# Reordering the first mixer and the memory attention of a two-block transformer kernel, and turning some projections round

## The reference, cut to what matters

```python
h = rms_norm(x, norm_mix[l])
z = h @ w_in[l]                      # 2048 x 5144
z_a, z_b, z_cq, z_ckv_c, z_ckv_s, z_ckv_w, z_cg = jnp.split(z, split_at, axis=-1)
out_a = spatial_gating(z_a, ...)     # gMLP
out_b = dilated_attention(...)       # 4 heads, from z_b: "attention B"
out_c = nsa_attention(...)           # 8 heads, 2 key groups, compressed keys: "attention C"
x = x + jnp.concatenate([out_a, out_b, out_c], axis=-1) @ w_out[l]
h = rms_norm(x, norm_xattn[l]); m = rms_norm(mem, norm_mem[l])
q = h @ xattn_wq[l]; kv = m @ xattn_wkv[l]        # memory attention, 4 heads: "attention X"
x = x + softmax_attention(q, kv) @ xattn_wo[l]
x = x + jnp.square(jax.nn.relu(rms_norm(x, norm_mlp[l]) @ w_up[l])) @ w_down[l]
# second block: its six modulation vectors are
jax.nn.silu(c) @ w_mod[l] + b_mod[l]              # w_mod: 2048 x 12288; the same for c_ctx
```

## Time and profile before

| what | value |
|---|---|
| median of 3 runs | 2880.22 us (2876.76 to 2888.32) |
| the profiled execution | 2886.28 us, span 2884.5 us |
| PE busy in the span | 2743.1 us (95%) |
| DVE, ACT busy | 1877.8 us (65%), 1266.7 us (44%) |
| DMA | 572.40 MB, mean 198 GB/s |
| mean granted TensorE clock | 0.976 |

### The profile page before, as it was taken

One profiled execution on the slowest core, in us unless ns is written; L12 is line 12 of the kernel. 1 busy time (PEld: TensorE's weight loads), 2 busy tenths in 40 slices (PEclk: granted clock), 3 DMA queues, 4 the chain that ended last, 5 costly groups with the idle time before them and its releaser, 6 DMA issues.

```text
span 2884.5 us, 32270 instructions
## 1 busy us (share of the span) xinstructions
PE 2743.1 (95%) x12593; PEld 2244.0 (78%) x12593; DVE 1877.8 (65%) x2476; ACT 1266.7 (44%) x1636; POOL 82.6 (3%) x78
## 2 busy tenths in 40 slices
PE   7889999889999999999899999988989999999999
PEld 6777887668888888788678877767768888888887
DVE  5676666767688888766645556666666666454555
ACT  5353334444444434345555535434454444434433
POOL 0000000000000000100000010100000000000000
PEclk9999989999999999999999999998999999999999
DMA  7667854637778777865556535434247777666665
GB/s 237 223 212 246 277 180 133 221 120 255 253 255 261 250 255 255 278 220 183 167 165 185 174 105 160 125 93 128 87 132 234 247 249 246 190 188 191 190 190 175
DMA packets 303619, 572.40 MB, mean 198 GB/s; under 512 B 20389, under 2 KB 30122, under 8 KB 303082
## 3 DMA queue, kind: packets, MB, share of 16 engines
q1 hardware_dynamic: 301434, 562.06, 62.2%
q0 software_dynamic: 2032, 8.26, 1.1%
HBM read 568.16 MB, written 2.10 MB: 198 GB/s over the span
## 4 chain that ended last, share of the span: by engine, by line
PE 80%; DVE 7%; ACT 5%; issue 4%; DMA 4%; POOL 0%; SPq 0%; DVEq 0%; ACTq 0%
PE ps L1444 24%; PE ps L1446 24%; PE ps L1445 23%; ACT whi L1696 2%; PE ps L1424 2%; DVE wlo L1964 1%; DMA raw<-in_w_in 1%; PE ps L1635 1%; PE ps L1655 1%; DVE yb L2012 1%; DVE acc L1982 1%; PE ps L1456 1%; DMA raw<-in_w_down 1%; ACT Eb L1765 1%; PE ps L1517 1%
## 5 line engine op out<-in xcount | busy, mean ns | idle before, releaser
L1964 DVE TENSOR_TENSOR wlo<-raw,whi 128x1024 fp32r<-128x1024 f32 x857 | 1046.9, 1229 | 667.9 <-ACT whi L1696 659.8
L1444 PE MATMUL ps<-whi,th 128*128 128x512 f32 (+1 forms) x3456 | 1388.0, 402 | 41.3 <-DVE wlo L1964 23.8
L1696 ACT ACTIVATE whi<-raw 128x1024 fp32r<-128x1024 f32 x857 | 900.0, 1057 | 1057.4 <-PE ps L1446 350.4
L1446 PE MATMUL ps<-whi,tl 128*128 128x512 f32 (+1 forms) x3456 | 1356.1, 392 | 0.0
L1445 PE MATMUL ps<-wlo,th 128*128 128x512 f32 (+1 forms) x3456 | 1355.6, 392 | 0.0
L1444 PEld LDWEIGHTS ps<-whi,th 128*128 128x128 f32 x3456 | 659.7, 191 | 184.4 <-DVE wlo L1964 33.9
L1446 PEld LDWEIGHTS ps<-whi,tl 128*128 128x128 f32 x3456 | 658.4, 191 | 140.5
L1445 PEld LDWEIGHTS ps<-wlo,th 128*128 128x128 f32 x3456 | 660.0, 191 | 132.2 <-issue 2.7
L1982 DVE SCALAR_TENSOR_TENSOR acc<-raw,silc,acc 128x512 f32<-128x512 f32 x480 | 355.4, 771 | 49.6 <-DMA raw<-in_w_mod 44.6
L1722 ACT ACTIVATE th<-yb 128x512 fp32r<-128x512 f32 x56 | 35.4, 632 | 135.4 <-DVE yb L2012 78.5
L1424 PE MATMUL ps<-ident,stg 128*128 128x128 f32 x344 | 54.4, 283 | 13.3 <-issue 4.3
(11 more groups left out here) (246 smaller groups left out, 1291.2 us busy)
## 6 DMA issues: line engine op xcount, KB each, us to landing
raw<-in_w_in SPq DMA_DIRECT2D x240, 512.0 KB, 3.8
raw<-in_w_down SPq DMA_DIRECT2D x216, 512.0 KB, 3.9
raw<-in_w_mod SPq DMA_DIRECT2D x192, 512.0 KB, 3.9
raw<-in_w_gate_up SPq DMA_DIRECT2D x176, 512.0 KB, 3.8
raw<-in_w_up SPq DMA_DIRECT2D x128, 512.0 KB, 4.1
raw<-in_w_out SPq DMA_DIRECT2D x64, 512.0 KB, 3.7
raw<-in_xattn_wkv SPq DMA_DIRECT2D x16, 512.0 KB, 5.3
raw<-in_xattn_wq SPq DMA_DIRECT2D x8, 512.0 KB, 4.2
```

The source lines that it names most:

```text
L1444: pe.matmul(p[:, 0:n], xh, wh[:, c, :], start=first and c == 0, stop=False)
L1446: ins = pe.matmul(p[:, 0:n], xl, wh[:, c, :], start=False, stop=last and c == len(kts) - 1)
L1696: self.e.activation(t.his[g % NHI][:, 0:n], t.raws[j % NRAW][:, 0:n], ACT.Copy).then_inc(*s.hi.up(g))
L1964: self.e.tensor_tensor(t.los[j % NRAW][:, 0:n], t.raws[j % NRAW][:, 0:n], t.his[g % NHI][:, 0:n].bitcast(F), ALU.subtract).then_inc(*s.lo. ...
```

## The change

- **Loads.** SP starts with x and the chunks; the identity and norm_mix go on ACT's queue, the other eleven small loads on POOL's. Only norm_mix is turned at the start; the rest (`columns_rest`) and x's sum of squares come in a new lane "load".
- **Order of the first mixer.** cc first (x is turned during it), then gMLP v and u, ck0, ck1, cg, cq0, cq1, bq, bk, bv. Attention C runs behind bq, bk and bv; attention B behind w_out. w_out's column blocks 0 and 1 are started without the rows of attention B (kts 0 to 3 and 8 to 15), both pairs of banks stay taken, and the rest is added when B is done; blocks 2 and 3 go over all rows at once. The separate residual additions of the first half are gone.
- **Memory.** POOL loads mem in four parts late in the first mixer; it is turned during w_out, with its squares on ACT (`mem_square`). Then come mk, the query xq, and mv; attention X's scores run during mv at two steps a chunk (`pace`), its values after mv.
- **Turned projections.** cc, cq0, cq1, bq, bk, mk and xq take the form "heads", ck0 and ck1 "both": 128 columns of the weight are the stationary operand and 256 tokens move past, so that the result lies in PSUM as head by token. A row of 1/rms, spread over the partitions by two PE products for each of x, xa and mem (`spread`), is multiplied in by DVE (`heads_direct`), and `heads_out` and `heads_turn` aren't used for these.
- **Turns of x.** The pieces wait `lag` ticks after a residual block (2 in w_out, 4 in wo; one before).
- **Modulation.** `mods_start(8, 16, 0.62)` after cc, none during w_out and the memory attention (rate 0), what is left of blocks 8 to 15 and blocks 0 to 7 in the MLP at 0.36, and blocks 16 to 19 at 0.2 in the second mixer's projections.
- **Others.** The hidden values are squared by ACT; the context is asked for one step earlier in the program, behind the same wait.

```diff
+            at = row0 + 128 * kts[i]
...
-                elif src is t.x and self.rn <= q:
-                    while self.rn <= q:
+                elif src == self.x_part:
+                    while self.rn <= q or self.ticks < self.rn_at[q] + lag:
+                        if self.rn > q and op.hurry:
+                            break
                         yield
-                    yield
...
+    def direct(self, name, dst, h0, by, nh=4, used=()):
+
         def epi(pair, end):
-            self.rows_out(rname, pair, end, rdst, 0, 256, 256, f, by, used)
-            self.flags.add(rname)
-            heads_epi(pair, end)
+            for b in range(nh // 2):
+                self.heads_direct(name, b, pair, end, dst[:, h0 + 2 * b:h0 + 2 * b + 2, :], by, used)
...
+        if "values" in A:
+            for i in range(n + 3):
+                for d, f in ((3, s3), (1, s2), (0, s1)):
+                    if 0 <= i - d < n:
+                        f(units[i - d])
+                yield
+            yield from self.until(A["values"])
+            for u in units:
+                s4(u)
+            yield
+            return
...
+        op1 = self.op1x = Operand(t.op["1"], [], "x")
+        self.turn("x", self.x_part, lambda q, tb: self.xb[2 * q + tb], None, op1, t.gain["mix"], None, [(s.cols, "mix")], lag=0)
...
+        def first_steps():
+            slot = self.side().take()
+            self.columns_rest(slot.tile)
+            slot.give((s.cols, "cols"), (s.cols, "cols2"), (s.cols, "bmc"))
+            self.stgs.after = [[(s.ini, "rest")], [(s.ini, "rest")]]
+            yield
+            yield
+            self.late_loads()
+            yield
+            op1.rs = self.stats("x", t.x, [w for v in self.xb for w in v], 2)
+            self.spread("x", op1.rs)
+            for _ in range(6):
                 yield
...
-        self.gemm(op2, w_kv, 0, 0, 512, range(16), self.heads("mk", t.mk, 0, ACT.Copy, by=op2))
...
-        self.gemm(op2, w_kv, 0, 512, 512, range(16), self.rows("mv", t.mv, 0, 512, 0, ACT.Copy, by=op2))
...
-        self.mods_start(8, 20, 0.62)
...
-        self.gemm(op1, w_in, 0, 1024, 512, range(16), self.heads("bq", t.bq, 0, ACT.Copy, by=op1))
-        self.gemm(op1, w_in, 0, 1536, 512, range(16), self.heads("bk", t.bk, 0, ACT.Copy, by=op1))
-        self.gemm(op1, w_in, 0, 2048, 512, range(16), self.rows("bv", t.bv, 0, 512, 0, ACT.Copy, by=op1))
...
+        self.gemm(op1, w_in, 0, 3584, 512, range(16), self.direct("cc", t.cc, 0, op1), "heads")
+        self.spawn("big", self.compress())
+        self.mods_start(8, 16, 0.62)
+        op2m = Operand(t.op["2"], [])
         self.gemm(op1, w_in, 0, 512, 512, range(16), self.gmlp_v)
         self.gemm(op1, w_in, 0, 0, 512, range(16), self.gmlp_uv(op2m))
...
+                      self.direct_and_rows(f"ck{i}", t.ckT[i], f"cv{i}", t.cv[i], op1), "both")
...
+        self.gemm(op1, w_in, 0, 2560, 512, range(16), self.direct("cq0", t.cq, 0, op1), "heads")
+        self.gemm(op1, w_in, 0, 3072, 512, range(16), self.direct("cq1", t.cq, 4, op1), "heads")
         self.spawn("big", self.probabilities())
...
+        scrC = self.scratch_of(attC)
+        self.gemm(op1, w_in, 0, 1024, 512, range(16), self.direct("bq", t.bq, 0, op1), "heads")
+        self.gemm(op1, w_in, 0, 1536, 512, range(16), self.direct("bk", t.bk, 0, op1), "heads")
+        self.gemm(op1, w_in, 0, 2048, 512, range(16), self.rows("bv", t.bv, 0, 512, 0, ACT.Copy, by=op1))
...
+        w_out, pairs = a["w_out"][0], []
+        self.rate = 0.0
+        for n in range(2):
+            pairs.append(self.take_pair())
+            self.part(op2m, w_out, 0, 512 * n, 512, [*range(4), *range(8, 16)], pairs[n], last=False)
...
+        def load_mem():
+            for q in range(3):
+                self.load_mem_part(q, free)
+            yield
+            yield
+            yield
+            self.turn("mem", mem_part, mem_key, None, opk, t.gain["mem"], None, [(s.cols, "cols")], rest=1)
+            for q in range(4):
+                for tb in range(2):
+                    self.mem_square(q, tb, mem_part(q, tb), mem_key(q, tb))
+                while opk.pieces < 2 * q + 2:
+                    next(opk.gen)
+                    yield
+                if q == 0:
+                    self.load_mem_part(3, [(s.tp, ("mem", 1)), (s.msq, (0, 1))])
+            self.reduce_sums("mem", t.st[:, 0:2], t.ssm, [(s.msq, (3, 1))])
+            self.root("mem", t.st[:, 0:2], D, [(s.rd, "mem")])
+            opk.rs = [(t.st[:, tb:tb + 1], (s.rs, "mem")) for tb in range(2)]
+            self.spread("mem", opk.rs)
+        self.spawn("load", load_mem())
...
+        opx = early_turn("xa", op1.end, t.gain["xa"], 2)
+        for n in range(2):
+            self.residual("mix", n, last=True)(pairs[n], self.part(op2m, w_out, 0, 512 * n, 512, range(4, 8), pairs[n], first=False))
+        for n in range(2, 4):
+            self.gemm(op2m, w_out, 0, 512 * n, 512, range(16), self.residual("mix", n, last=True))
...
+        self.drain("load")
+        w_kv = a["xattn_wkv"][0]
+        self.gemm(opk, w_kv, 0, 0, 512, range(16), self.direct("mk", t.mk, 0, opk), "heads")
+        self.gemm(opx, a["xattn_wq"][0], 0, 0, 512, range(16), self.direct("xq", t.xq, 0, opx), "heads")
...
+        self.pace = 2
+        self.gemm(opk, w_kv, 0, 512, 512, range(16), self.rows("mv", t.mv, 0, 512, 0, ACT.Copy, by=opk))
+        self.pace = 1
...
-        opm = early_turn("mlp", opx.end, t.gain["mlp"])
-        self.rate = 0.0
+        opm = early_turn("mlp", opx.end, t.gain["mlp"], 4)
...
+        self.rate = 0.36
...
+            if b == 3:
+                self.load_ctx(opm.end)
...
+        self.mods_start(16, 20, 0.2)
...
+        heads = {"rows": 0, "heads": n // 128, "both": n // 256}[form]
+        c0 = 128 * heads
...
+            for h in range(heads):
+                p, hs = pair.tile[h // 2][:, S * (h % 2):S * (h % 2) + S], slice(128 * h, 128 * h + 128)
+                pe.matmul(p, wh[:, c, hs], op.h[:, kt, :], start=a and h % 2 == 0, stop=False, skip_group_check=True)
+                pe.matmul(p, wl[:, c, hs], op.h[:, kt, :], start=False, stop=False, skip_group_check=True)
+                ins = pe.matmul(p, wh[:, c, hs], op.l[:, kt, :], start=False, stop=z, skip_group_check=True)
...
+        for tb in range(2):
+            self.wait_ge(*self.s.u0.at((key, tb)))
+            self.e.activation(slot.tile[:, tb, :], slot.tile[:, tb, :], ACT.Square).then_inc(*self.s.u1.up((key, tb)))
...
+    def heads_direct(self, name, b, pair, end, dst, by, used):
+        t, s = self.t, self.s
+        self.wait_all([end])
+        self.wait_ge(*s.sd.at(by.name))
+        self.wait_all(used)
+        self.e.tensor_tensor(dst, pair.tile[b][:, :].rearrange("p (a b) -> p a b", a=2),
```

More of the change, by code:

```diff
@@ L351, in tick @@
     def tick(self):
+        self.ticks += 1
         self.step("small")
-        self.step("big")
+        for _ in range(self.pace):
+            self.step("big")
+        self.step("load")
         self.step("mod")
@@ L668, in s4 @@
             h = heads[u["h"]]
-            bank = (self.own if self.own.ready() else self.big).take()
+            bank = (self.own if self.own.ready() and "values" not in A else self.big).take()
             self.att_values(A, u, bank, h["pt"], h.get("pc"))
@@ L1069, in run @@
-        self.spawn("big", self.after(self.attention(attB), "bq", "bk", "bv"))
+            next(op1.gen)
+        self.spawn("small", op1.gen)
+        def first_steps():
[10 more added lines that the diff above has]
+            for _ in range(6):
+                yield
+            slot = self.side().take()
+            self.spatial_weights(slot)
+            slot.give((s.wt, 0))
@@ L1106, in early_turn @@
             return op
-        opx = early_turn("xa", op1.end, t.gain["xa"])
-        for n in range(4):
-            self.gemm(op2m, w_out, 1024, 512 * n, 512, range(8, 16), self.residual("mix1", n, last=True))
-        opx.rs = self.sums("xa", 4)
-        self.gemm(opx, a["xattn_wq"][0], 0, 0, 512, range(16), self.heads("xq", t.bq, 0, ACT.Copy, by=opx, used=scrC))
-        self.drain("small")
+        opk = Operand(t.op["3"], scrB + scrC, "mem")
+        mem_key = lambda q, tb: [(s.ld_mem[q], 0)]
@@ L1150, in run @@
         self.acc_after[2] = self.acc_after[3] = scrX
[L1151 to L1152 removed]
+        self.rate = 0.36
+        self.todo = self.todo + [(j, kc) for j in range(8) for kc in range(8)]
         ho = up(0)
```

333 lines of the change are left out of this document (194 added, 139 removed).

## The result

The changed kernel takes 2864.52 us (2859.78 to 2868.94, 7 runs) where the kernel before takes 2880.22 (2876.76 to 2888.32, 7 runs): a ratio of 0.9942, interval 0.9925 to 0.9958. It is faster by 15.7 us, where 41 were forecast. The range of 2806 to 2876 holds it, the forecast's own range of 2818 to 2860 does not.

A forecast was written before the change was run, and what follows sets the result against it. PE, busy for 95% of the span, was taken as the bound, with 107 us lost in the first 650 us. Terms of -57.4 and +16 made -41: 2845 from the profiled 2886.28, so 2839 us predicted, own range 2818 to 2860.

The forecast's parts named there:

- Part 1: Kernel start: with x loaded first, the chain to the first product begins 5.7 us earlier, -5.7 us.
- part 3: Turned projections: 1728 matmuls of 256 columns at 113 ns each, load hidden, cost 0; bounds -5 and +12 us.
- parts 5 and 6: Attention B moved from beside gMLP behind w_out, -10.5 us; attention C under 24 chunks instead of 16, -6 us.
- parts 7 to 9: Fewer waits in w_out, -6 us; in query and attention X, -7; in wo, -7.
- Rival A: Weight loads don't hide, so a turned matmul takes 223 ns: about 3029 us; with other slowdowns, chance 0.10.
- rival D: Fixed 13 ns per matmul, so a turned one takes 120 ns, +12 us: 2851 us; chance 0.60 together with the forecast.
- Part 9: wo: the 4.27 us wait for x goes with a lag of 4, -7 us of 9.3.
- Part 11: MLP: three leftover modulation steps, twelve additions in a heap before down(3), make PE wait, +4 us, bounds 0 and +8.
- Part 12: Second mixer: 32 modulation steps, 49 us of new DVE work, a sixth of it exposed: +8 us, bounds 0 and +20.
- Part 13: DMA: compression right behind cc plus modulation, 45.6 MB taking 155 us, close to even with PE: +4 us, bounds 0 and +10.
- Rival B: Waits move and don't go: parts 4 to 9 give -15 instead of -46 us, 2870 us in all; chance 0.16.
- parts 4 to 9: Waits removed in turning x, attentions B and C, w_out, query with attention X, and wo: 46 us won together.

The follow-up runs named there:

- b_mod: Kernel before with only modulation blocks 16 to 19 moved from first block and MLP into the second mixer at 0.2: 2874.49 us, ratio 0.9969.
- d_keep: Changed kernel with lag 3 into the MLP, compression eight chunks later, modulation continued at 0.62 in w_out, MLP rate 0.32: 2864.76 us, ratio 0.9937.
- a_rows: Changed kernel with cc, cq0, cq1, bq, bk, mk and xq back to tokens stationary, staged copies and transposes: 2872.88 us, ratio 0.9968.
- a_split: Changed kernel with the first eight MLP products in matmuls of 256 columns instead of 512, tokens still stationary: 2871.75 us, ratio 0.9969.
- a_lag2: Changed kernel with the pieces of x for the MLP 2 ticks behind the residual instead of 4: 2857.13 us, ratio 0.9919.
- a_rate: Changed kernel with the MLP's modulation rate at 0.38 instead of 0.36: 2852.82 us, ratio 0.9902.
- b_mlp: Changed kernel with modulation blocks 16 to 19 in the MLP (115 steps at 0.53), none in the second mixer: 2862.88 us, ratio 0.9928.
- c_late: Changed kernel with MLP rate 0.38, lag 2, compression eight chunks later, and blocks 16 to 19 begun behind the context's products at 0.25: 2853.42 us, ratio 0.9896.
- b_comp: Changed kernel with the compression started eight chunks later, behind gMLP's v product: 2859.25 us, ratio 0.9917.

## Why the prediction came out as it did

**Held.** Part 1: the first product starts 5.7 us earlier. Parts 4 to 8 and 10: parts 1 to 10 and 13 sum to -53.4 us by the start of the MLP, and the mark is -54.1. That agreement is luck. It holds 11.6 us too little for part 3, and about 6 that are the profiled execution of before and not the change. Without these two the other parts won some 59 us (66 if the 6 stay in) where -57.4 + 4 = -53.4 were forecast. The waits of the old order went for the most part (parts 5 and 6 had kept 8 and 6 us of them): 0 to 563 us, which is all that lies ahead of the MLP, loses 51 us after, 35.2 idle and 15.8 to the clock. In the first 600 us, where near 60 were forecast, it is 69, as the MLP's first waits are in it.

b_mod and d_keep show what I had not put in any part: in the kernel before, modulation in the second half of w_out and the memory attention cost 14 us by itself. My parts 7 to 9 named it as one reason among others. With the turned form at 8 to 11 (a_rows) and the start at 5.7, what is left of 48, some 17 to 20, goes to the order if the parts add up, which no run shows.

Rival A fell: turned matmuls are 120 ns apart, not 223. The Trainium skill, "TensorE: Matmul & The Clock Gate", Part 3, "The mechanism", would have loads wait unless they target other row groups; the rows at 225 us speak against it for this stream, in which all loads take all rows.

**Part 3, mis-sized.** I took 113 ns and a cost of 0; rival D's fixed 13 ns holds, 1728 x 6.7 = 11.6 us. a_split shows that it does not hang on which operand is stationary. Half of 227 ns was the wrong choice, as it shares the 13 ns that the earlier trace rows already had above 512/2.4 between two matmuls. The same page of the Trainium skill, Part 1, "Wait — 56ns, not 53.3ns?", gives a fixed cost of about 2.5 ns a matmul at 2.4 GHz, in a section whose example is bf16. Here it is 13 (227 - 213.3 and 120 - 106.7).

**Part 9, wrong.** This is the step that failed in its mechanism, and not only in size. The lag of 4 wins in wo what it should (5.6 us of the 7), but I put nothing in the sum for what is late next. The pieces held back meet the first product of the MLP: PE waits 2.03, 6.00 and 3.53 us for `tl`, 11.6 in all, and the mark goes from -54.1 to -43.0. a_lag2 has none of this loss (-48.5 to -48.9) and is 6.6 us faster. With part 3 it is the largest error, 11 us.

**Part 11, mis-sized.** The heap of twelve additions came at 1230 us as predicted, but cost 8.3 us by the marks for 4. I priced the wait (4.8 us forecast, 2.8 in the trace) and left out the fall of the clock behind it, 3.4 us. The sixteen small products at 1238 us come in a_rate too, where they take 1.84 us for 2.40. That is some 7 of the 8.3; the rest is not assigned. a_rate removes all of it, for 0.02 of a step per chunk.

**Part 12, mis-sized.** 13.2 us for 8, within its bound of 20. b_mlp, which has no step there, wins 2.1 in the same stretch, so the modulation costs 15. The same stretch costs 14.1 in b_mod, on top of the kernel before. The sixth of DVE's 49 us that I took as exposed was nearer to a third. Six of them lie not in the scan, where I had looked, but in the first 16 chunks: there the scaling of x by its 1/rms and gain on DVE, the square of the result on ACT, rounding and rest take turns, 4.3 us a chunk for PE's 2.72. The timeline of DVE after has:

```profile
1349.68 1.41 DVE L2366 SCALAR_TENSOR_TENSOR x<-x,st,gt 128x512 f32<-128x512 f32 x2
...
1353.97 1.41 DVE L2366 SCALAR_TENSOR_TENSOR x<-x,st,gt 128x512 f32<-128x512 f32 x2
```

b_mlp goes round at the same 4.3 us without any step (1357.24, 1361.54 and 1365.83), so the round is not the modulation's; it uses up the lookahead, and the steps that start there then fall on PE. That last link is argued; c_late, which starts its steps behind the context, loses 0.9 us there for 6.2.

**Part 13, right in size by luck.** +4 forecast; b_comp shows 3 to 7 us for the early compression. But it is one wait of 7.95 us at 55 us and the slow clock behind it, not traffic that falls short over 155 us, as I had worked it out.

Summed over the profiles: -41 as forecast, +11.6 (part 3), +11.1 (part 9), +4.3 (part 11), +5.2 (part 12), and -12.3 for what the other parts won up to the MLP beyond their forecast, make -21; measured -23.4. About half of the -12.3 is the 6 us of the profile of before: without them the sum is -15, and the medians say -15.7. Rival B, by which waits move rather than go, forecast -10 and so was nearer to -15.7 than my -41. It was right as to what happens, but not where: parts 4 to 9 gave at least their 46 us and not a third of it, as near as the marks tell, and the waits moved out of the stretch that the change rearranges, into the MLP and the second mixer. What the first 16 chunks of the second mixer would cost with a deeper lookahead was not tried.

## What to carry to other kernels

When work is held back or moved to relieve one stretch, follow it to where it lands: each of the three losses here lay just behind the stretch that the change had cleared, and two of them went by changing one number. The same step of work, 1.5 us of DVE, had very different prices by where it stood: little in most of the MLP at 0.38 to 0.40 steps a chunk (before loses 1.3 us over 540), but 8 us in all for those that meet the load of the context there; 0.5 to 0.6 us for each one added at 0.45 to 0.53; 0.3 to 0.7 in the second mixer; and 1.0 to 1.3 of its 1.5 beside attention and transposes in w_out, though DVE was busy for 72% there and 81% in the MLP of b_mlp. So price a moved step by the chain that it enters, and not by the engine's spare share. And before a difference of two profiles is explained, look how far apart two executions of the same instructions are: here 5 to 6 us, as much as some of the effects.

## What the runs showed of the hardware

A float32r matmul with its weight load costs about 13 ns beyond its columns at 2.4 GHz, at both sizes that were read and whichever operand is stationary: 227 ns at 512 columns, 120 ns at 256 in both forms. The load of 128 columns before each of them fits into those 120 ns. At 1.2 GHz the 13 ns don't show: three matmuls of 512 columns take 1160.80 - 1159.52 = 1.28 us there, 427 ns each, and 512/1.2 is 427. Timeline of PE after, at a granted clock of 0.50:

```profile
1159.52 0.63 PE L1578 MATMUL ps<-whi,th 128*128 128x512 f32 x1
...
1160.80 0.57 PE L1578 MATMUL ps<-whi,th 128*128 128x512 f32 x1
```

In the MLP of b_mlp 1.53 chunks of 512 KB are read for each one multiplied. With its transposes and sums a chunk takes 2.89 us where PE doesn't wait (before rounds 187 in the 540 us), which asks for 278 GB/s, and 295 while the twelve matmuls of 2.72 us run. The core gets 274 and PE idles 14.5 us; at 1.40 chunks, in before, it moves 254 and idles 1.3. It is no ceiling of the rate, since before moved 295 GB/s over 50 us without idle time of PE; which transfers were late and why was not tried.
